# A load queue, the roundings' places and the experts' pages rearranged in a two-layer fp32 kernel

## What is computed

```python
# first block: x, ctx are (1, 256, 1024)
sh_m, sc_m, g_m, sh_f, sc_f, g_f = adaln(c, ada_w, ada_b)          # silu(c) @ (1024 x 6144); the same for c_ctx
h     = modulate(rmsnorm(x), sh_m, sc_m);  h_ctx = modulate(rmsnorm(ctx), csh_m, csc_m)
q, ff, fb, v, g, u, sv, ga, gb = split(h @ w_in)                    # w_in 1024 x 5632; f, b, v for h_ctx too
o     = gated linear attention, forward and backward over the tokens, from the context's final state
y     = sigmoid(ga) * (rmsnorm(o) * silu(g) @ w_a) + sigmoid(gb) * (sgu(u, sv) @ w_b)
x     = x + g_m * (y @ w_out)
h2    = modulate(rmsnorm(x), sh_f, sc_f)
aff   = softmax(h2 @ router_w)                                      # 16 experts, each takes its 32 best tokens
ye    = (silu(xs @ wg[e]) * (xs @ wu[e])) @ wd[e]                   # wg, wu 1024 x 2048, wd 2048 x 1024, for e in 16
x     = x + g_f * scatter(ye * gate)
# second block: a gated linear attention, a convolution branch, a merge, an embedding gate, a final norm
```

## Time and profile before

| | |
|---|---|
| median of 3 runs | 1647.25 us (1646.15 to 1648.4) |
| the profiled execution's own time | 1646.58 us |
| its span | 1644.8 us, so 1.8 us lie around it |
| TensorE busy | 1229.9 us, 75% |
| DVE busy | 565.3 us, 34% |
| ACT busy | 420.9 us, 26% |
| moved by DMA | 520.92 MB, mean 317 GB/s |

### The profile page before, as it was taken

The page is one execution under the profiler, slowest core; times in us unless marked ns, Lnnn a source line. Parts: engine busy times, 40 slices in busy tenths (PEclk is TensorE's granted clock), DMA queues, the critical chain, the costliest instruction groups (busy, mean ns, idle before and its releaser), DMA issues.

```text
span 1644.8 us, 18879 instructions
## 1 busy us (share of the span) xinstructions
PE 1229.9 (75%) x8264; PEld 754.7 (46%) x8264; DVE 565.3 (34%) x815; ACT 420.9 (26%) x541; POOL 36.6 (2%) x39
## 2 busy tenths in 40 slices
PE   4977789898766665666566566666656799999997
PEld 1746788884221111111111111111111399999996
DVE  4637697442110110111011011011101377767565
ACT  3534456422100000000000000000000345367544
POOL 0002210000000000000000000000000000000000
PEclk8988899898987877788788887678787799999998
DMA  9872233389999999999999999999999745455551
GB/s 369 314 256 65 77 104 128 129 342 387 428 420 428 427 428 427 428 429 428 427 428 428 427 428 428 428 428 428 428 428 427 290 146 162 154 180 179 185 189 37
DMA packets 121648, 520.92 MB, mean 317 GB/s; under 512 B 7248, under 2 KB 91216, under 8 KB 93792
## 3 DMA queue, kind: packets, MB, share of 16 engines
q1 hardware_dynamic: 121424, 519.64, 79.1%
q10 hardware_dynamic: 144, 0.09, 0.0%
HBM read 518.66 MB, written 1.05 MB: 316 GB/s over the span
## 4 chain that ended last, share of the span: by engine, by line
DMA 51%; PE 37%; DVE 7%; ACT 2%; issue 2%; SPq 1%; DVEq 0%; ACTq 0%
DMA pair<-in_wu 20%; PE B L1483 16%; DMA pair<-in_wd 15%; DMA pair<-in_wg 14%; PE B L1487 8%; PE B L1791 4%; DMA wslot<-in_w_in 3%; DVE wslot_r L837 2%; PE B L1835 1%; PE B L1759 1%; ACT whi L449 1%; PE B L1459 1%; DVE PT L937 1%; SPq L345 0%; PE B L1815 0%
## 5 line engine op out<-in xcount | busy, mean ns | idle before, releaser
L1791 PE MATMUL B<-pair,xs 128*32 128x512 f32 x2048 | 316.8, 748 | 204.4 <-DMA pair<-in_wu 127.1
L1791 PEld LDWEIGHTS B<-pair,xs 128*32 128x32 f32 x2048 | 63.9, 123 | 429.6 <-issue 177.2
L1835 PE MATMUL B<-pair,hidT 128*32 128x512 f32 x1008 | 179.1, 848 | 98.4 <-DMA pair<-in_wd 91.5
L1835 PEld LDWEIGHTS B<-pair,hidT 128*32 128x32 f32 x1008 | 33.4, 134 | 226.8 <-DMA pair<-in_wd 146.8
L837 DVE TENSOR_TENSOR wslot_r<-wslot,whj 128x2048 fp32r<-128x2048 f32 x52 | 118.9, 2288 | 38.2 <-ACT whj L449 38.2
L449 ACT ACTIVATE whj<-wslot 128x2048 fp32r<-128x2048 f32 x52 | 99.3, 1912 | 96.1 <-PE B L1487 90.5
L1483 PE MATMUL B<-hnh,whj 128*128 128x256 f32 x496 | 122.6, 285 | 0.0
L1483 PE MATMUL B<-hn_r,whj 128*128 128x256 f32 x496 | 121.5, 283 | 0.0
L1151 DVE COPY ye<-B 128x512 f32<-128x512 f32 x16 | 11.1, 691 | 295.7 <-PE B L1835 295.7
L1127 DVE SCALAR_TENSOR_TENSOR x<-B,mod,x 128x256 f32<-128x256 f32 x128 | 55.9, 479 | 148.2 <-PE B L1775 148.2
L1147 DVE TENSOR_TENSOR hid<-sgm,B 128x512 f32<-128x512 f32 x16 | 11.0, 687 | 254.1 <-PE B L1791 254.1
(11 more groups left out here) (433 smaller groups left out, 1880.8 us busy)
## 6 DMA issues: line engine op xcount, KB each, us to landing
pair<-in_wg SPq DMA_DIRECT2D x64, 2048.0 KB, 41.4
pair<-in_wu SPq DMA_DIRECT2D x64, 2048.0 KB, 40.9
pair<-in_wd SPq DMA_DIRECT2D x63, 2048.0 KB, 41.0
wslot<-in_w_in SPq DMA_DIRECT2D x58, 1024.0 KB, 5.2
aslot<-in_ada_w SPq DMA_DIRECT2D x20, 1024.0 KB, 7.6
wslot<-in_ada_w SPq DMA_DIRECT2D x4, 1024.0 KB, 9.1
wslot<-in_w_out SPq DMA_DIRECT2D x4, 1024.0 KB, 5.1
wslot<-in_wa SPq DMA_DIRECT2D x4, 1024.0 KB, 5.6
```

Source lines behind the costliest of these rows:

```text
L1791: mm = e.matmul(B[b][32 * j:32 * j + 32, :], XS[:, k, 32 * x:32 * x + 32], tile_at_page(t)[:, 512 * j:512 * j + 512], start=k == 0, stop=k ...
L1835: mm = e.matmul(B[3 + db][32 * c:32 * c + 32, :], hidT[:, 128 * c + 32 * j:128 * c + 32 * j + 32], v2(tile_at_page(t + c // 2))[:, c % 2, ...
```

## The change

1. In SP's queue tiles 5, 6, 7 and 8 are issued ahead of pieces of the condition that they stood behind; the waits of the pieces are spread between the tiles.
2. ACT's `hi` and DVE's `lo` move behind the work of the same step. In the gate heads: behind the exponential and behind the product. In the levels: `hi` to the end of ACT's step, `lo` from the end of a level into the middle of the next (between line 915 and the wait for ACT's exponential). Where two units are squared, ACT squares both before it makes a sigmoid.
3. The router's small products on DVE move ahead of the C gates.
4. The experts' pages are handed out in the order of `PAIRS`, as pairs. The first five pairs of expert 0 are loaded in the middle of the first block: two when o is done, one when u is done, two after C. To make room the activations `h` and `ctx` change places, and the merged values move from `h` to `wtok` and `ctx`.

```diff
@@ memory
-        XC0 = put("ctx", 2048)
-        XC = v8(XC0)
         HT0, HTl0 = both("h", 4096)
+        XC_at = pos[0]
+        XC = v8(put("ctx", 2048))
...
-        MGh = v8(put("mgh", 2048, m_at, FR))
+        MGh = v8(put("mgh", 2048, XC_at, FR))
...
-        MG, MGl = HT[:, :, 0:256], HTl[:, :, 0:256]
+        MG, MGl = SB, v8(MGl0)
@@ pages of the experts
-        RING = [BASE + i for i in range(6)] + list(range(4)) + [BASE + i for i in range(6, MORE)]
-        RN = len(RING)
...
-        STAND_IN = {RN - 2: 4, RN - 1: BASE + MORE + AUX}
+        zpair = lambda i: BASE + i
+        TURN = [zpair(2), zpair(4), zpair(12), zpair(0), zpair(6), 0, 2, zpair(8), zpair(10)]
+        EXTRA = BASE + MORE + AUX
+        PAIRS = TURN[:2] + [EXTRA] + TURN[3:] + TURN[:2] + TURN[3:]
+        PAIRS += [TURN[i % 9] for i in range(12 * NE - len(PAIRS))]
+        tile_page = lambda t: PAIRS[t // 2]
@@ sync
             ada(1, 3)
+            weights(5)
             e.dma_start(wtok0[:, 0:1152], a["msk"]).then_inc(*l_msk())
             e.wait_ge(*p_proj.at("tile", 0))
             weights(4)
-            for k in range(4, 8):
-                e.wait_ge(*p_ada.at(1, k - 4))
-                ada(1, k)
-            weights(5)
-            for k in range(4):
-                e.wait_ge(*p_ada.at(1, k + 4))
-                ada(2, k)
             e.wait_ge(*p_proj.at("tile", 1))
             weights(6)
...
+            e.wait_ge(*p_ada.at(1, 1))
+            ada(1, 4)
+            ada(1, 5)
+            e.wait_ge(*p_proj.at("tile", 2))
+            weights(7)
...
+                if n == NO["A", 0] + BASE:
+                    e.wait_ge(*p_misc.at("o", 3))
+                    experts(0)
+                    experts(2)
+                if n == NO["A", 3] + BASE:
+                    e.wait_ge(*v_mid.at("uT"))
+                    experts(4)
+                if n == NO["C", 3] + BASE:
+                    experts(6)
+                    experts(8)
...
-                elif t >= RN:
-                    e.wait_ge(*p_exp.at("tile", t + 1 - RN))
+                elif before(t) is not None:
+                    e.wait_ge(*p_exp.at("tile", before(t)))
@@ scalar, gate heads
-                    if h % 2:
-                        hi(NO["FB"[d], h // 2] + 3)
                     sigmoid(f, "f", d, h)
...
                     e.activation(f[:, 0:256], cu[:, 0:256], ACT.Exp, bias=last, scale=-1.0).then_inc(*a_h("decay", d, h))
+                    if h % 2:
+                        hi(NO["FB"[d], h // 2] + 3)
@@ scalar, levels
                     hh = li - 6
+                    sigmoid(pair(gT, hh), "g", hh)
                     hi(NO["G", hh] + 3)
-                    sigmoid(pair(gT, hh), "g", hh)
@@ vector, gate heads
                     clamp(f, B_of["f", d, h], "f", d, h)
-                    if h % 2:
-                        lo(NO["FB"[d], h // 2] + 3)
...
                     e.tensor_tensor(wctx[:, 4 * d + h, :], cu[:, 256:512], f[:, 0:256], ALU.mult).then_inc(*v_mid("w", d, h))
+                    if h % 2:
+                        lo(NO["FB"[d], h // 2] + 3)
@@ vector, levels
                 e.tensor_tensor(K_[:, :, 1, :], rb, B_[:, :, 1, :], ALU.subtract).then_inc(*v_lvl(li))
+                if rest is not None:
+                    lo(rest)
                 e.wait_ge(*a_lvl.at("k", li))
@@ vector, router
-            for i in range(4):
-                gates("C", i)
...
                 e.tensor_tensor(w, wr, ffs[:, at:at + 8].rearrange("p (k o) -> p k o", o=1).broadcast_to([128, 8, 16]), ALU.mult).then_inc(*v_mid("router", at))
+            for i in range(4):
+                gates("C", i)
```

More of the change, by code:

```diff
@@ L141, in program @@
         vc, gT = v2(vc0), v4(vc0)
-        wtok0 = put("wtok", 2048)
+        wtok0, MGl0 = both("wtok", 2048)
         wtok, SB = v2(wtok0), v8(wtok0)
@@ L280, in program, with before @@
         ada_src = lambda q, k: a["ada_w"][k * 128:(k + 1) * 128, q * 2048:(q + 1) * 2048]
-        RING = [BASE + i for i in range(6)] + list(range(4)) + [BASE + i for i in range(6, MORE)]
-        RN = len(RING)
-        PLE_AT = 48
-        STAND_IN = {RN - 2: 4, RN - 1: BASE + MORE + AUX}
-        tile_page = lambda t: STAND_IN[t] if t in STAND_IN else RING[t % RN]
-        pairs = {r: put(f"pair{r}", 2 * SLOT, (slots_at if r < BASE else zone - BASE * SLOT) + r * SLOT) for r in RING[::2]}
-        tile_at_page = lambda t: slots[STAND_IN[t]] if t in STAND_IN else pairs[tile_page(t - t % 2)][:, t % 2 * SLOT:t % 2 * SLOT + SLOT]
+        zpair = lambda i: BASE + i
[3 more added lines that the diff above has]
+        PAIRS += [TURN[i % 9] for i in range(12 * NE - len(PAIRS))]
+        PLE_AT = 48
+        tile_page = lambda t: PAIRS[t // 2]
+        pairs = {r: put(f"pair{r}", 2 * SLOT, page(17) if r == EXTRA else slots_at + r * SLOT if r < BASE else page(r - BASE)) for r in set(PAIRS)}
+        tile_at_page = lambda t: pairs[tile_page(t)][:, t % 2 * SLOT:t % 2 * SLOT + SLOT]
+        last_tile = lambda r: max(2 * i + 1 for i in range(12 * NE) if PAIRS[i] == r)
+        def before(t):
+            earlier = [i for i in range(t // 2) if PAIRS[i] == PAIRS[t // 2]]
+            return 2 * earlier[-1] + 1 if earlier else None
         def expert_src(t):
@@ L392, in sync @@
-            for n in range(7, SECOND):
+            e.wait_ge(*p_ada.at(1, 1))
[3 more added lines that the diff above has]
+            weights(7)
+            e.wait_ge(*p_ada.at(1, 3))
+            ada(1, 6)
+            ada(1, 7)
+            e.wait_ge(*p_ada.at(1, 5))
+            ada(2, 0)
+            ada(2, 1)
+            e.wait_ge(*p_proj.at("tile", 3))
+            weights(8)
+            e.wait_ge(*p_ada.at(1, 7))
+            ada(2, 2)
@@ new lines, in sync @@
+            ada(2, 3)
+            e.wait_ge(*p_ada.at(2, 1))
+            ada(2, 4)
+            ada(2, 5)
+            e.wait_ge(*p_proj.at("tile", 4))
+            weights(9)
+            e.wait_ge(*p_ada.at(2, 3))
+            ada(2, 6)
+            ada(2, 7)
+            e.dma_start(iot, a["iota"]).then_inc(*l_iot())
+            e.dma_start(wst, a["wst"].rearrange("g s t -> s g t")).then_inc(*l_wst())
+            e.dma_start(flat(bsb), a["sgu_b"].rearrange("(o g) t -> o (g t)", o=1).broadcast_to([128, 512])).then_inc(*l_bsb())
@@ L393, in sync, with experts @@
+            e.dma_start(wr, a["router_w"].rearrange("(k p) n -> p k n", p=128)).then_inc(*l_wr())
+            def experts(t):
+                e.dma_start(pairs[tile_page(t)], expert_src(t)).then_inc(*landed[tile_page(t)]("expert", t))
+            for n in range(10, SECOND):
                 e.wait_ge(*p_proj.at("tile", n - BASE))
                 weights(n)
-            for t in range(0, 24 * NE, 2):
+                if n == NO["A", 0] + BASE:
[8 more added lines that the diff above has]
+                    experts(8)
@@ L397, in sync @@
+            for t in range(10, 24 * NE, 2):
                 if t == PLE_AT:
-                    e.wait_ge(*p_exp.at("tile", RN - 2))
                     e.dma_start(wpp, a["wpp"].rearrange("(k p) n -> p k n", p=128)).then_inc(*l_pp())
@@ L403, in sync @@
                     e.dma_start(kn8(gkw0), a["w_in2"].rearrange("(k p) n -> p k n", p=128)[:, :, 3072:3088]).then_inc(*l_gw())
[L404 to L408, removed]
+                if t in (10, 12):
+                    e.wait_ge(*p_proj.at("tile", SECOND - BASE + t - 9))
+                elif t == 14:
                     e.wait_ge(*p_proj.at("wo", 3))
-                elif t == 2 * RN - 2:
+                elif before(t) is not None:
+                    e.wait_ge(*p_exp.at("tile", before(t)))
+                elif tile_page(t) == zpair(12):
                     e.wait_ge(*a_moe.at("xs", 1, 7))
-                elif t >= RN:
-                    e.wait_ge(*p_exp.at("tile", t + 1 - RN))
[L414 to L418, removed]
+                experts(t)
             for n in range(SECOND, NT):
                 if n < SECOND + 4:
-                    e.wait_ge(*p_exp.at("tile", 24 * NE - RN + n - SECOND))
+                    e.wait_ge(*p_exp.at("tile", last_tile(tile_slot(n) // 2 * 2)))
                 elif n == SECOND + 4:
@@ L997, in vector @@
                 scores(li)
-                lo(NO["V", 0] + li + 3)
+            lo(NO["A", 0] + 3)
             flush()
@@ L1830, in tensor @@
                     t = 24 * x + 16 + 2 * j
-                    for u in (t, t + 1) if t in STAND_IN else (t,):
-                        e.wait_ge(*landed[tile_page(u)].at("expert", u))
+                    e.wait_ge(*landed[tile_page(t)].at("expert", t))
                     for db in range(2):
```

41 lines of the change are left out of this document (17 added, 24 removed).

## The result

The changed kernel takes **1636.38 us** (median of 4 runs, 1635.51 to 1637.74) against 1647.32 (4 runs): a ratio of 0.9934, 95% interval 0.9917 to 0.9952, so 10.9 us faster. The prediction was 1634 (1625 to 1641). The profiled execution took 1636.6 us with a span of 1634.8.

The account below looks back on a forecast made before the run. Expert bytes, locked behind the first expert matmul, bound the kernel: 9.8 + 1.5 + 5.2 = 16.5 us earlier, stream 4 longer, so 1646.58 - 12.5 = 1634.1, median 1634.8, taken as 1634; range 1625 to 1641 (8 in 10).

Parts of the forecast that it names:

- Stream bound from the first expert matmul: Expert stream: 366 of 384 tiles, 897 us at 428 GB/s, wait behind the first expert matmul; only its shift moves the end.
- Gates, 9.8 us: Gate heads: no landing wait remains, a pair takes 16.2 us, levels start at 132.8 instead of 142.58; bounds 4 and 14.
- slower rival: Gate heads: tiles 5 to 7 still land late and the new order adds 11 us, giving 1655; chance 0.05.
- Levels, 1.5 us: Levels: moved `lo` and joint squares save 9.1 us, DVE's waits for `hi` cost 7.6; between -1.5 and 9.
- Router, 5.2 us: Router: the small product's operand is ready before C, so 5.16 us of idle TensorE go; bounds 3 and 5.2.
- Stream's start, a loss of 4 us: Start of the expert stream: the new page order makes tile 24 wait for tile 9, leaving a hole; bounds 0 and 5.5.
- Early pairs hidden: First block: the expert pairs loaded early delay no weight tile beyond its cover, so they cost nothing.
- Tail unchanged: From last landing to end: unchanged, as second-block tiles go out about 7 us later but behind some 30 us of loads.
- the prefetch is the gain: Expert stream: bytes are the bound from 329 on, so five early pairs take off 24.5 us, giving 1622; chance 0.04.
- roundings cost nothing in the levels: Levels: GpSimd's slowing and slack swallow the waits for `hi`, so they give 9 us, time 1627; chance 0.15.
- expert pairs ahead of a weight tile stall TensorE: A, C or w_out: early expert pairs delay weight tiles by up to 9.8 us, giving 1644; chance 0.08.

Follow-up runs that it names:

- gate roundings back: The changed kernel with the roundings of the q and gate heads back in their old places, all else as changed: 1627.35 us, ratio 0.9878.
- no prefetch: The changed kernel with the first five expert pairs issued only after the last dense weights, not during the first block: 1637.21 us, ratio 0.9935.
- all three: The changed kernel with the pages' old order, q and gate roundings in old places, and `hi` ahead of the sigmoids in the levels: 1613.17 us, ratio 0.9793.
- old page order: The changed kernel with the pages' old order, so t=22 and 24 wait for tiles 5 and 7 again: 1632.55 us, ratio 0.9909.
- `hi` first: The changed kernel with ACT's `hi` ahead of the sigmoids in the levels again, `lo` still in the middle of the level: 1626.21 us, ratio 0.9869.
- order alone: The kernel before with only the roundings at q and in the gate heads moved behind their activations, old load order: 1638.44 us, ratio 0.9942.
- loads alone: The kernel before with only the new load order of tiles 5 to 9 and the condition's pieces: 1628.44 us, ratio 0.9881.
- router back: The changed kernel with the C gates ahead of the router's products again: 1643.39 us (10 runs), ratio 0.9976.

## Why the prediction was right

The time (1634 against 1636.4) and the mechanism held, but two terms of the sum were off by about 2 us each and nearly cancelled, which is luck. Term by term:

- **Stream bound from the first expert matmul:** held in all ten kernels, as the table shows.
- **Gates, 9.8 us:** measured 9.1 at the first difference (133.50 against 142.58, 132.8 predicted) and 9.9 at the first scores. A pair of heads is 16.16 us (16.2 predicted). The load order by itself brings 18.0 at the scores, and the order of the roundings takes 8.3 back. That is less than the 11 put down for it in the slower rival, since without it TensorE bounds the stage. The working put that bound at 131, and the scores came at 130.95, but its terms (113, 3 and 12) add up to 128. With the gate roundings back, the eight heads end at 117.7: the row copy costs a wait of 2.66 us, products of 1.12 us and, behind the wait, a slow clock (0.50 from 93 to 95 us). So the 131 is luck too.
- **Levels, 1.5 us:** the mis-sized term. From the first scores to o they gave 0.3, and o itself lost 1.1: A1's first matmul starts at 247.56 instead of 256.72, so the stage gave -0.8. The waits for `whi` have about the sizes that were written down: six before o, 1.1 to 1.6 and 2.64 us, 9.5 in all, where I had 10.6 (a seventh, 2.67, comes when o has begun). The 3 us that I took off for slow differences don't show: the place of `hi` costs 10.1, where I had 7.6 net. And behind the last of the six, TensorE stands still for 5.89 us and makes o partly at the low clock. With no such waits the levels give 10.4, where I had 9.1 (9 as the bound).
- **Router, 5.2 us:** it gave 7.05. The idle time was right; the 1.8 us that the same products take less behind no idle time were left out. This nearly pays for the levels, which I had not foreseen: 9.9 - 0.8 + 7.05 = 16.15, against 16.5 predicted and 16.05 measured.
- **Stream's start, a loss of 4 us:** 4.5, with the hole 19 to 24 us after the first expert matmul, and gone with the old order.
- **Early pairs hidden:** held. Leaving them out changes nothing that the measurement can tell.
- **Tail unchanged:** 351.7 us from last landing to the end, against 350.1, so the sum lost 1.6 us that it did not have. They lie in the first 20 us behind the last landing, and they are TensorE's clock: the second block's first dense product starts 19.8 to 20.1 us behind the landing in the three kernels with a tail of about 350 (before, no prefetch, all three), where the mean granted clock of these 20 us is 0.91, and 21.6 to 21.8 us behind it in the seven with about 351.7, where it is 0.74 or 0.83. From there on all ten take the same time within 0.2 us. The kernels before and with the old page order have the same idle times on TensorE there within 0.3 us, and still part. So the 1.6 us are no work of the change that these runs show; what makes the clock differ is open.

Over the profiled executions the change gave 9.98 us (1646.58 to 1636.6) where the sum had 12.5: 0.45 less at the first expert matmul, 0.5 more for the stream, 1.6 more for the tail. (The sum ends at 1634.8, and 1634 was taken.)

The hole's size rests on the rate. At 428 GB/s three pairs last 14.7 us, and by that the loss was to be 4. The windows after show 428 again, and the loss was 4.5.

The Trainium skill (page "DMA: Bandwidth & Descriptors", section "Where 436 GB/s comes from") puts the HBM side's limit at about 358 GB/s for a core, by which the prediction estimated a loss of 2.5. The trace does not agree, by its 428. The Trainium skill says on the same page, section "Measured (HBM→SBUF, 128 partitions, SWDGE, issued from GpSimd)", that about 358 is what each core gets when both cores of an HBM domain stream; this kernel's program runs on one core, so the measured 428 does not speak against that sentence.

Of the rivals, that the prefetch is the gain is excluded by the kernel without it (1637, not 1650), and that roundings cost nothing in the levels by the kernel with `hi` first. That expert pairs ahead of a weight tile stall TensorE is excluded by the kernel without them as well: its o, its router products and its first expert matmul start at 238.66, 291.28 and 365.94, within 0.1 us of the kernel after. The slower rival's mechanism, that the order's price comes on top of late landings, is excluded too: order alone, with the late loads, gives 1638.44. There my working of the price was incomplete. I had put a landing and the work of a head one behind the other, and they overlap once the rounding stands behind that work.

## What to carry to other kernels

When a rounding or copy waits for a landing, moving the load up and moving the rounding down are two ways to remove the same stall. Their gains didn't add here (18.0 and 9.5 us at the first scores alone, 9.9 together), and the rounding in the late place has a price of its own on the engine that needs it next; try each alone before both. A single change that nets little can hold large parts of both signs: here the moved loads, `lo` in mid-level with the joint squares, and the router's order gave, and `hi` late, the gate order and the page order took back 23 of 34 us. Where a ring of pages feeds a stream that is bound by its bandwidth, look at which tile each of the first few refills waits for: here that alone decided the stream's length (912.6 or 917), and filling the ring sooner won nothing.

## What the runs showed of the hardware

- **Idle time can cost twice on TensorE.** The same 16 products (line 1694) take 1.96 us with no gap ahead and a granted clock of 1.00 (2.4 GHz), and 3.60 us behind 5.17 us of idle time, at 0.50 (1.2 GHz). The first scores take 3.78 us behind 8.48 us idle, and 2.05 us behind 1.10 us idle (loads alone). The last gap alone does not tell which it will be: before the change the first scores took 3.65 us behind only 2.16 us, at a granted clock of 0.57 from 149 to 153.
- **Profiles of one program part by the clock.** The kernel after and the one with the router back have one and the same program up to the A gates and agree to 0.1 us at the first scores (139.25 and 139.35). Then they part by 2.4 us at the second scores, with the same idle times on the way. The windows from 158.3 to 162.3, of the kernel after first:

```profile
158.30:162.30 4.00, 4.00 (x37) 4.00 (x37) 0.00 (x0) 1.69 (x3) 0.00 (x0) 1.00 0.31 102
```

```profile
158.30:162.30 4.00, 3.80 (x20) 3.73 (x21) 0.00 (x0) 1.83 (x4) 0.00 (x0) 0.59 0.52 176
```

  In the second the granted clock is 0.59, and 20 products are done in place of 37. A difference of 2 us between two profiles of this kernel is therefore no evidence of a cause in the code.
